# A 32-expert mixture stage of a Trainium2 program: experts written out, thirteen weight buffers, token rows gathered and scattered by GpSimd

## The reference, cut to what matters

```python
rows = jnp.zeros((n_blocks * MOE_BLOCK, d), h.dtype).at[dest].set(h[tok_sorted])

def expert_block(args):
    xb, e = args
    return (jax.nn.silu(xb @ w_gate[e]) * (xb @ w_up[e])) @ w_down[e]

out = lax.map(expert_block, (rows.reshape(n_blocks, MOE_BLOCK, d), block_expert)).reshape(-1, d)
contrib = (out[dest] * gate_sorted[:, None]).astype(h.dtype)
return jnp.zeros((n_tok, d), h.dtype).at[tok_sorted].add(contrib)
```

## Time and profile before

| what | value |
|---|---|
| median of 3 runs | 3686.52 us (3684.63 to 3698.89) |
| the profiled execution's own time | 3695.86 us |
| its span, first to last instruction | 3694.0 us |
| granted TensorE clock, mean of the span | 0.947 |
| PE, PEld busy | 3314.0 us (90%), 2695.1 us (73%) |
| DVE, ACT, POOL busy | 2268.0 us (61%), 1461.0 us (40%), 190.8 us (5%) |
| moved by DMA | 526.26 MB, mean 142 GB/s |

### The profile page before, as it was taken

The page is one execution under the profiler, slowest core; times in us unless marked ns, Lnnn a source line. Parts: engine busy times, 40 slices in busy tenths (PEclk is TensorE's granted clock), DMA queues, the critical chain, the costliest instruction groups (busy, mean ns, idle before and its releaser), DMA issues. The chain is left out here.

```text
span 3694.0 us, 47797 instructions
## 1 busy us (share of the span) xinstructions
PE 3314.0 (90%) x18602; PEld 2695.1 (73%) x18602; DVE 2268.0 (61%) x2957; ACT 1461.0 (40%) x1921; POOL 190.8 (5%) x147
## 2 busy tenths in 40 slices
PE   7998899999999988899999788899869959999994
PEld 5886688888887977777778588796648746666662
DVE  6467647666564257577765365764632448788883
ACT  5216613222122146432333243433322237777771
POOL 0020000000000000000000043211100000000000
PEclk8999989999999999999999899999979969999997
DMA  6640013444432211266541080110023169999992
GB/s 231 208 135 12 1 50 122 159 137 137 156 119 60 64 62 41 72 190 204 188 155 52 16 234 1 35 47 24 18 63 85 52 242 349 376 371 389 378 381 85
DMA packets 355820, 526.26 MB, mean 142 GB/s; under 512 B 15056, under 2 KB 292176, under 8 KB 330064
## 3 DMA queue, kind: packets, MB, share of 16 engines
q1 hardware_dynamic: 349776, 503.21, 40.2%
q10 hardware_dynamic: 3584, 12.58, 0.9%
q0 software_dynamic: 2304, 8.39, 0.6%
HBM read 484.81 MB, written 39.32 MB: 142 GB/s over the span
## 5 line engine op out<-in xcount | busy, mean ns | idle before, releaser
L267 DVE TENSOR_TENSOR lo<-exp_raw,exp_hi 128x2048 fp32r<-128x2048 f32 x192 | 436.3, 2287 | 107.0 <-ACT exp_hi L3280 106.5
L3280 ACT CAST exp_hi<-exp_raw 128x2048 fp32r<-128x2048 f32 x192 | 366.9, 1913 | 158.9 <-DMA exp_raw<-in_w_experts 77.0
L260 PE MATMUL ffn_acc<-normed_hi,up_w_hi 128*128 128x512 f32 (+1 forms) x1056 | 378.1, 358 | 9.5 <-DVE lo L646 6.1
L261 PE MATMUL ffn_acc<-lo,up_w_hi 128*128 128x512 f32 (+1 forms) x1056 | 377.9, 358 | 0.0
L260 PEld LDWEIGHTS ffn_acc<-normed_hi,up_w_hi 128*128 128x128 f32 x1056 | 199.8, 189 | 43.5 <-issue 6.7
L418 DVE SCALAR_TENSOR_TENSOR aside_w<-aside_w,aside_c 128x1024 f32<-128x1024 f32 x176 | 210.0, 1224 | 28.6 <-DMA aside_w<-in_ada_t 20.6
L261 PEld LDWEIGHTS ffn_acc<-lo,up_w_hi 128*128 128x128 f32 x1056 | 200.6, 190 | 32.3
L260 PE MATMUL ffn_acc<-gated_hi,down_w_hi 128*128 128x512 f32 (+1 forms) x528 | 190.9, 362 | 17.0 <-DVE lo L267 17.0
L262 PE MATMUL ffn_acc<-normed_hi,up_w_lo 128*128 128x512 f32 (+1 forms) x528 | 190.1, 360 | 0.0
L261 PE MATMUL ffn_acc<-lo,down_w_hi 128*128 128x512 f32 (+1 forms) x528 | 189.6, 359 | 0.0
L1295 ACT ACTIVATE conv<-ffn_acc,vecs 128x768 f32<-128x768 f32 (+1 forms) x88 | 73.2, 882 | 291.6 <-PE ffn_acc L262 291.6
(11 more groups left out here) (558 smaller groups left out, 8598.9 us busy)
## 6 DMA issues: line engine op xcount, KB each, us to landing
exp_raw<-in_w_experts SPq DMA_DIRECT2D x192, 1024.0 KB, 10.8
aside_w<-in_ada_t SPq DMA_DIRECT2D x176, 512.0 KB, 6.2
up_w<-in_ffn_up SPq DMA_DIRECT2D x88, 512.0 KB, 5.2
x_rows<-dn_zero SPq DMA_DIRECT2D x42, 384.0 KB, 5.3
exp_x<-x_rows SPq DMA_DIRECT2D x32, 384.0 KB, 6.8
y_rows<-exp_y ACTq DMA_DIRECT2D x32, 384.0 KB, 8.0
ada_w<-in_ada_first SPq DMA_DIRECT2D x8, 1024.0 KB, 12.2
v<-in_ada_t SPq DMA_DIRECT2D x16, 512.0 KB, 6.7
```

The source lines that it names most:

```text
L260: nc.tensor.matmul(out, left[0], right[0], start=start, stop=False)
L261: nc.tensor.matmul(out, left[0], right[1], start=False, stop=False)
L267: return engine.tensor_tensor(lo, value, hi.bitcast(F32), ALU.subtract)
L3280: nc.scalar.copy(hi[r][:], raw[u * TILES + j][:]).then_inc(tile_hi[j], 1)
```

## The change

It does seven things.

1. The loop over pairs of experts is gone: all 32 experts are written out on every engine. The extra blocks keep their loop, with semaphores of their own (`x_more`, `y_more`).
2. There are 13 buffers `raw`, used as a ring in the order in which PE uses the tiles (`turns`: gate and up of expert e, then down of e-1). SP loads the next tile each time PE is done with one.
3. Tokens are no longer loaded by SP, nor results stored by ACT. POOL gathers the rows of block e with an indirect DMA and scatters the results with another; the index of a row that holds no token is set beyond the tensor (`filled`, four small DVE instructions), and such rows are out of bounds for `bounds_check`.
4. Two memsets on POOL clear the token buffers once, and all 42 blocks of `y_rows` are zeroed rather than 10: 84 zeroing DMAs on SP in the delta-net stage, not 52.
5. `exp_xhi` and `exp_xlo` have two buffers each. PE turns the tokens of e+1 between gate and up of e, and ACT and DVE split them ahead of the next expert's tiles.
6. The first expert's down is put behind up of the second, and gate of the second before `turn_hidden` of the first.
7. 20 matmuls of 128 x 512 in float32 (WARM) follow the last routing matmul on PE; nothing reads their result.

```diff
-TILES, TILE = 6, 2048
+TILES, TILE, TILE_RING = 6, 2048, 13
+WARM = 20
...
-            for rows, first in ((K.x_rows, 0), (K.y_rows, NE)):
-                for b in range(first, NE + NOVER):
+            for rows in (K.x_rows, K.y_rows):
+                for b in range(NE + NOVER):
...
-            xr = [K.sb(ex, f"exp_x{u}", [MB, D]) for u in range(2)]
-            xh, xl = (K.sb(ex, "exp_x" + n, [P, KD, MB], FR) for n in ("hi", "lo"))
+            xh, xl = ([K.sb(ex, f"exp_x{n}{u}", [P, KD, MB], FR) for u in range(2)] for n in ("hi", "lo"))
...
+        turns = []
+        for e in range(NE + 1):
+            turns += [(e, j) for j in GATE + UP if e < NE] + [(e - 1, j) for j in DOWN if e >= 1]
...
+            for e, j in turns[:TILE_RING]:
+                tile_in(e, j)
+            for n, (e, j) in enumerate(turns[TILE_RING:]):
+                sp.wait_ge(used, n + 1)
+                tile_in(e, j)
...
+            for u in range(2):
+                nc.gpsimd.memset(xr[u][:], 0.0).then_inc(blank, 1)
...
+            def block_rows(e):
+                return bass.IndirectOffsetOnAxis(ap=filled[0:MB, e:e + 1], axis=0)
+
+            def tokens_in(e):
+                nc.gpsimd.indirect_dma_start(out=xr[e % 2][:], out_offset=None, in_=x_rows, in_offset=block_rows(e),
+                                             bounds_check=NSL - 1, oob_is_err=False).then_inc(x_full[e % 2], 16)
+
+            def store(e):
+                nc.gpsimd.indirect_dma_start(out=y_rows, out_offset=block_rows(e), in_=y[e % 2][:], in_offset=None,
+                                             bounds_check=NSL - 1, oob_is_err=False).then_inc(y_stored[e % 2], 16)
+
+            pool.wait_ge(filled_ready, 1)
+            pool.wait_ge(blank, 2)
+            pool.wait_ge(routed, 16 * TOPK * NTX)
+            for e in range(2):
+                tokens_in(e)
+            for e in range(2, NE + 2):
+                if e < NE:
+                    pool.wait_ge(x_turned, e - 1)
+                    tokens_in(e)
+                if e >= 3:
+                    pool.wait_ge(y_out, e - 1)
+                    store(e - 3)
+            pool.wait_ge(y_out, NE + 1)
+            store(NE - 1)
...
+            pe.wait_ge(rows_out, NTX)
+            for n in range(WARM):
+                nc.tensor.matmul(tp[:, 0, 0:512], ident, K.consts[:, 0:512], start=True, stop=True)
...
+            ts(unused[:], cnt[:], K.const("blk"), float(2 * NSL), ALU.is_le, ALU.mult)
+            dve.drain()
+            nc.vector.scalar_tensor_tensor(unused[:], K.const("slot0"), K.const("blk"), unused[:], ALU.add, ALU.add)
+            dve.drain()
+            nc.vector.tensor_copy(filled[:], unused[:]).then_inc(filled_ready, 1)
...
             turn(0, 0)
...
+            gate(0, 0)
+            turn(1, 1)
+            lift(0, 0)
+            pe.wait_ge(silu, 1)
+            gate(1, 1)
+            turn_hidden(0)
+            for e in range(1, NE):
+                if e >= 2:
+                    gate(e, e)
+                if e + 1 < NE:
+                    turn(e + 1, (e + 1) % 2)
+                lift(e, e)
+                down(e - 1, e - 1)
+                turn_hidden(e)
+            down(NE - 1, NE - 1)
```

More of the change, by code:

```diff
@@ L2905, in _, with moe @@
             pair(KD // 2 - 1, False)
-def moe(K, h, w_router, w_experts, x_rows, y_rows, gate, dest, blocks, raw, sc):
+def moe(K, h, w_router, w_experts, x_rows, y_rows, gate, dest, filled, blocks, raw, sc):
     nc = K.nc
@@ L2952, in moe @@
             y = [K.sb(ex, f"exp_y{u}", [MB, D]) for u in range(2)]
+            xr = [K.sb(ex, f"exp_x{u}", [MB, D]) for u in range(2)]
         with ExitStack() as pc:
@@ new lines, in up_tile, with gate, lift, down @@
+                last.then_inc(used, 1)
+            def gate(b, e):
+                pe.wait_ge(x_split, b + 1)
+                for j in GATE:
+                    up_tile(b, e, j, gp)
+            def lift(b, e):
+                for j in UP:
+                    up_tile(b, e, j, up)
+            def down(b, e):
+                pe.wait_ge(h_split, b + 1)
+                pe.wait_ge(y_out, b + 1)
+                for j in DOWN:
+                    pe.wait_ge(tile_lo[j], b + 1)
+                    for c in range(KE // 2):
+                        k = (j % 2) * KE // 2 + c
+                        for n in range(2):
+                            last = products(nc, yp[0:MB, n * 512:(n + 1) * 512], (hh[:, k, :], hl[:, k, :]),
+                                            weights(e, j, slice(c * D + n * 512, c * D + (n + 1) * 512)), k == 0, k == KE - 1)
+                    last.then_inc(used, 1)
@@ L3333, in _ @@
[L3333 to L3344 removed]
+            for j in UP:
+                hi_tile(0, j)
+            for e in range(NE):
+                if e >= 1:
+                    for j in DOWN:
+                        hi_tile(e - 1, j)
+                if e == 1:
+                    act.wait_ge(hid_turned, 1)
+                activate(turn_of[e, GATE[1]] + 1)
+                if e + 1 < NE:
+                    hi_tokens(e + 1, (e + 1) % 2)
+                    for j in GATE + UP:
+                        hi_tile(e + 1, j)
+                if e >= 1:
+                    finished(e - 1)
+                hi_hidden(e)
@@ L3345, in _ @@
+            for j in DOWN:
+                hi_tile(NE - 1, j)
+            finished(NE - 1)
             n = n_over(act)
@@ L3414, in _ @@
+            for j in DOWN:
+                lo_tile(NE - 1, NE - 1, j)
             n = n_over(dve)
@@ L3529, in second_block @@
             blocks = K.sb(rt, "blocks", [1, NOVER + 1], I32)
-            raw = [K.sb(rt, f"exp_raw{r}", [P, TILE]) for r in range(2 * TILES)]
+            filled = K.sb(rt, "filled", [P, NE], U32)
+            raw = [K.sb(rt, f"exp_raw{r}", [P, TILE]) for r in range(TILE_RING)]
             with ExitStack() as sc:
```

322 lines of the change are left out of this document (114 added, 208 removed).

## The result

The changed kernel takes 3662.81 us (median of 4 runs, 3661.34 to 3663.79); the kernel before takes 3690.06 (4 runs, 3684.63 to 3698.89). The ratio is 0.992, with a 95% interval of 0.9902 to 0.9937. The profiled execution took 3661.34 us, with a span of 3659.5, against 3695.86 and 3694.0.

The account below looks back on a forecast made before the run. It took DMA transfers (18.3 us an expert against PE's 17.66) as the bound. Terms -29.3 - 7.0 + 1.5 + 1.4 = -33.4 us gave 3662.5 for the profiled execution, 3653 for the median after 9.3 off; range 3643 to 3677.

Parts of the forecast that it names:

- the gain of 33.4: Whole kernel: sum of all terms, -33.4 us against the profiled execution's 3695.9, giving 3662.5 before the 9.3 taken off.
- Fewer bytes: Steady expert rhythm: 6.55 MB instead of 7.08 per expert makes PE the bound, 18.67 to 17.66 us each, -29.3 us.
- Ring: Weight-tile loads in order of use: makes the gain in the expert rhythm possible, no term of its own.
- Token split: Expert rhythm: transposes between gate and up, cast ahead of tile casts; PE's inputs at least 3 us early, own term nothing.
- if the cover goes: Expert rhythm: should the moved token split lose its time in hand, `exp_hid` on DVE would be late next; no size.
- The first experts: First gate matmul to expert 2's gate: 38.55 us falls to 31.5, -7.0 us; bounds -8.7 and 0.
- WARM: 20 matmuls before the first tokens: 9 to 17 us, pause 4 to 13, no gain or cost; bounds 0 and -2.4 us.
- First tokens and last store by POOL: Both ends of the expert stage: first gather costs +1.5 us, last result's store +1.4; bounds for each 0 and +3.
- POOL in the rhythm: Expert rhythm: two indirect DMAs per expert take at most 5 of 17.66 us on POOL and cost nothing.
- the rival in which VectorE waits for GpSimd: Expert rhythm: POOL's DMAs lengthen DVE's work; at 2.44 us each the pace is 20.3, time 3730 us; chance 0.07.
- Transfers stay the bound: Rival, expert rhythm: out-of-bounds rows cost like filled ones, pace 18.3 us, gain 14.8, time 3672 us; chance 0.10.
- Fetches and zeroing: Written-out code's some 24 fetches and 32 more zeroing DMAs: nothing; rival that fetches stop PE, 3689 us, chance 0.05.

Follow-up runs that it names:

- e2_few_rows_before: Kernel before, with token loads and stores of first blocks moving 32 rows instead of 96 and all 42 blocks of `y_rows` zeroed (output incomplete): 3667.35 us.
- e6_two_sets_all: Changed kernel with GpSimd moving all 96 rows and 12 weight buffers in two sets, loads in the old order: 3669.38 us.
- e1_all_rows: Changed kernel with the index of unused rows kept inside the array, so GpSimd gathers and scatters all 96 rows: 3665.87 us (ratio to the kernel before 0.9938).
- e5_old_split: Changed kernel with the token split back at its old place: one pair of split buffers, transposes behind up, cast behind the gate's casts: 3673.65 us.
- e9_plain_all: Changed kernel with all 96 rows loaded by SP and stored by ACT; ring of 13, written-out order and new token split kept: 3705.24 us.
- e13_plain_old_split: Changed kernel with all 96 rows moved by SP and ACT, ring of 13, and the token split back at its old place: 3698.12 us.
- e14_plain_few: Changed kernel with rows moved by SP and ACT, only 32 rows of a block (rows 32 to 95 of first blocks left out): 3654.39 us.
- e11_tail: Changed kernel with the last expert's down tiles cast and split ahead of what waits for down of the expert before: 3659.93 us.
- e10_plain_two_sets: Changed kernel with all 96 rows moved by SP and ACT and 12 weight buffers in two sets by the expert's parity, old load order: 3719.72 us.

## Why the prediction was right, and where not

**The forecast (3653, 3643 to 3677, faster).** 3662.81 is in the range and faster by more than 0.5%. It is 9.8 us above the point, and nearly all of that is one step: "the median of the runs is 9.3 lower, and I take the difference off at the end". The changed kernel's profiled execution (3661.34) was its fastest, not its slowest. And the 3686.52 of three runs was low: in the three later sets the kernel before had medians of 3690.4, 3690.0 and 3691.9, its second profiled execution 3695.53. Without this step the forecast would have been 3662.5.

That does not make the gain of 33.4 right. It was summed for the profiled pair, which differs by 34.5; the medians differ by only 27.3 (3690.06 and 3662.81). Both profiled executions of the kernel before lie some 5.5 us above its medians, the changed kernel's 1.5 below. In the second profile of the kernel before the rhythm took 538.98 us, which would make its gain 26.6 and not 29.15. How long the rhythm takes in an execution near the median no trace here shows.

**Fewer bytes, -29.3.** Measured -29.15, with PE as the bound. The bytes are enough for it (e2_few_rows_before), but the argument "7.08 MB at 386 GB/s, hence 18.3 us" took 386 GB/s for a ceiling. With the rows on GpSimd's queue the engines moved 397, not by more per share (395 at 1.02 is 388 at 1.00) but because the share went above the 0.98 that I had read as full.

**Ring, "none of its own".** Right for the changed kernel. With all the bytes it is worth 5.9 us (e6_two_sets_all against e1_all_rows), and the thirteenth buffer nothing.

**Token split, nothing in the rhythm.** Right (e5_old_split). But "if the cover goes, `exp_hid` on DVE is late next" was wrong: where the cover went, `exp_x` was late. The cover is the token load's short way by GpSimd, or a short queue. Beside loads of 96 rows on SP the two profiles put a price of 11.0 us on it in the rhythm (565.06 against 554.05, e9_plain_all and e13_plain_old_split), and a gain of 6.0 in the first experts (31.26 against 37.28); the medians leave the sum of the two open, as said above.

**The first experts, -7.0.** -6.4. Of it 4.7 is the split's new place (e5_old_split). I kept 1.7 us for matmuls at half speed, as before; there were twelve, not eight.

**WARM, nothing.** Right as it stands. But the earlier trace rows was misread: its 16 rows are 8 matmuls, two records each, so 20 matmuls take some 22 us by that row, and took 19.8, not 9 to 17; PE's pause behind them was 3.64 us, not 4 to 13. It cost nothing because the tokens came still later. The bound I gave, -2.4, may be low: in e14_plain_few the first tokens' row and the stretch behind it are 0.7 + 2.4 = 3.0 us shorter than in the changed kernel, though only 0.7 + 1.5 = 2.1 shorter than in e9_plain_all, which loads by SP as well.

**First tokens and last store by POOL, +1.5 and +1.4.** The stretches grew by 2.0 and 2.3 us. Of the kernels with WARM and the index in place, those that load all 96 rows by SP have their first tokens 55.4 to 55.7 us behind the router's load, those that gather 56.4 to 57.1, so the gather costs 0.7 to 1.7. At the other end, from gate(31) to the first gather of `combine`, kernels that store by ACT need 42.0 to 43.1 us and those that store by GpSimd 44.2 to 44.9 (e11_tail aside), so the store costs 1.1 to 2.9. Both bounds of the forecast hold.

**POOL in the rhythm, nothing.** The timeline of POOL and DVE shows the pattern of each expert:

```profile
3302.66 1.40 POOL L3044 DMA_INDIRECT y_rows<-exp_y,filled  x1 [13.14 <-ACT exp_y L3328]
3304.37 2.82 POOL L3040 DMA_INDIRECT exp_x<-x_rows,filled  x1 [0.30 <-issue]
...
3304.06 2.29 DVE L268 TENSOR_TENSOR lo<-exp_raw,exp_hi 128x2048 fp32r<-128x2048 f32 x1 [0.34 <-ACT exp_hi L3310]
3306.84 2.29 DVE L268 TENSOR_TENSOR lo<-exp_raw,exp_hi 128x2048 fp32r<-128x2048 f32 x1 [0.49 <-ACT exp_hi L3310]
```

The gather takes 2.82 us where it took 0.95 to 0.99 ahead of the first experts: it sits through a `lo`. `lo` takes 2.29 us as before, in every one of its rows from 3060 to 3560. One store DMA, the first, took 5.10 us, and PE waited for nothing. So the rival in which VectorE waits for GpSimd did not come, and the Trainium skill's rule ("SBUF — State Buffer", section "Who interferes with whom") showed in one direction only.

**Transfers stay the bound.** It did not come, since rows out of bounds move no bytes. But had they moved, e1_all_rows shows that 3672 would have been about 3666. The 358 GB/s of the Trainium skill ("SBUF — State Buffer", section "A bandwidth-pool intuition that's wrong (but worth ruling out)"), by which the same number came out, is no ceiling here: from 3060 to 3550 the kernels move 359 to 396 GB/s, and e1_all_rows holds 395. The Trainium skill ("Perfetto Trace Analysis", section "Roofline", in its note on HBM use over 100%) allows a core that runs alone more than its share, bounded by its 16 DMA engines at about 435 GB/s; the 419 GB/s of the earlier trace rows lie between the two.

**Fetches and zeroing, nothing.** No gap of PE stands in the rhythm, though instructions are fetched there now (18 packets on q8 from 3060 to 3550, where the kernel before had 2). `feat_w` is issued at 2246.7 and first read at 2324.3. The router's load starts within 0.5 us of before, which says little beside its 7 us from run to run.

## What to carry to other kernels

Where two resources both look full, a rate read at a DMA share of 0.98 is the rate of that mix of queues and not a ceiling: try the small urgent transfers on another queue (here GpSimd's was the only one tried) beside counting bytes. When a reader is moved ahead, look at the queue that its input stands in: with the rows on GpSimd's queue the edit cost nothing in the rhythm, and with the old loads on SP's (e10_plain_two_sets) PE waited for tokens 25 times. And forecast against the execution whose rows were summed; a correction to the median of three runs carries their luck along, and an excess of the old kernel's profile need not be there in the new one's.

## What the runs showed that I had not expected

The same 7.08 MB per expert moved at 397 GB/s with rows on GpSimd's queue and at 356 to 361 in a deep SP queue, both at a share of 1.01 to 1.02; a share of 1 does not say how much moves. Behind warm-up matmuls and a pause of 1.10 us the first experts started at full speed, 2.1 to 3.0 us shorter than with pauses of 2.24 and 3.64; with 3.64 the warm-up brought nothing that can be told from run to run.
